# Second layer's first conditioning columns: from beside the first layer's projection to beside its gates

## The chip, the cores and the metric

The kernel runs on one core of one Trainium2 chip. The metric is the device time of one execution in microseconds; less is better. The engines are TensorE (PE in the rows; PEld is its weight load), VectorE (DVE), ScalarE (ACT), GpSimd (POOL) and SyncE (SP), whose queue issues almost all transfers.

## What is computed

A stack of two transformer blocks follows another of two. The change touches the first. Its two layers work on 512 tokens of `x` and 256 of `ctx`, with 1024 columns:

```python
mod_x = (silu(c) @ w_ada[l] + b_ada[l])            # sh1, sc1, g1, sh2, sc2, g2
mod_c = (silu(c_ctx) @ w_ada[l] + b_ada[l])
p_x = modulate(x, sh1, sc1) @ w_in[l]              # keys/values, Fourier, queries, gate logits
g_f, g_m, g_g = split(sigmoid(gate_logits + b_gate), 3)
mix_x = (g_f * y_f + g_m * y_m + g_g * y_g) @ w_o
x = layer_norm(alpha * x + g1 * mix_x, ...)
x = layer_norm(alpha * x + g2 * sq_relu_mlp(modulate(x, sh2, sc2)), ...)
```

`w_ada[l]` is 1024 x 6144. Its six parts of 1024 columns are the six conditioning vectors. Each is needed for `c` and, in the first layer, for `c_ctx`. The second layer's parts 0 and 1 (`sh1`, `sc1`) are first needed at the end of the first layer's MLP.

## The kernel before

**Weight products.** `gemm` (line 313) runs a product as n slots over two ring buffers. In a slot TensorE works through G groups of tokens (the matmuls are line 367). It waits for the slot's weights (`ring_full`), for the pieces of their split (`w_split`), and, before group g, for the eviction of the group `depth` before it (`evac_done`). Each weight is split into a rounded part and a rest, so that three products of fp32r stand for one of fp32: lines 393 and 397 on VectorE, 395 and 397 on GpSimd. SP issues the weights of slot s + 2 when all groups of slot s are done (`mm_done`, lines 326 to 338). All orders are written out by hand; each engine's queue runs in program order.

**Conditioning units.** Most of `w_ada` is multiplied away from `gemm`, by the class `Macs` (line 516). A unit is 512 columns of one part of one layer. It is loaded in four quarters of 512 KB by SP (`load`, line 564) into two buffers: the load of quarter n waits until quarter n - 2 has been used (`mac_freed`). VectorE multiplies and adds a quarter with two k-tiles for each conditioning (`pieces`, line 573), so a unit with both conditionings is 16 operations on 512 columns: two `tensor_scalar` (line 587) and fourteen `scalar_tensor_tensor` (line 589, two inputs in SBUF). TensorE then sums over the partitions (`pe`, line 595): 8 matmuls with one column for the parts that go to columns (16 records, line 607), or a product with a 2-column pick for the parts 2 and 5 that go to rows (line 603). VectorE adds the sum to its place (`take`, lines 619 and 624). Parts 2 and 5 are also stored to memory, with their bias loaded first (lines 540 and 559). SP's part of a unit is the method `sp` (line 542): quarters 2 and 3 of this unit, the store of the unit before, the bias, and then quarters 0 and 1 of the next unit.

**Projection.** `project` (line 804) runs in each layer with four slots of 320 columns (G = 6, weights split by VectorE in four pieces) after a first product with two slots of 272. In the first layer the four slots also carry the four units of the second layer's parts 0 and 1: after a slot's split VectorE takes the unit before and works all four quarters of its own (lines 399 to 401); TensorE sums the unit of the slot before ahead of group 1. The last unit is summed after the last slot, and TensorE waits until it has been added. `fourier` comes next. Ahead of the units' loads SP issues the two loads of `fourier_loads` (2.1 MB).

**Gates.** `gated` (line 1567) runs eight slots. In the first layer G is 6: groups 0 to 2 are the three branches for 512 tokens, groups 3 to 5 for the other 256. A group is 24 fp32r matmuls and 4 of fp32 (8 records). The weights of a slot are six loads, and GpSimd splits them in six pieces of two operations once all six have landed. After each group ScalarE takes the sigmoid (line 1589) and VectorE multiplies and adds (lines 1606, 1608, 1611). `depth` is 3. Each slot carries one unit of the layer's own parts 2 to 5: after group 1 VectorE takes the unit of the slot before and works quarters 0 and 1, after group 2 quarters 2 and 3. TensorE sums the unit of the slot before ahead of group 1. In the second layer G is 3, with one conditioning. The eighth unit is summed and taken in `mix_norm` (line 1665), the output projection.

Of the kernel before, what the change touches and what calls it, by code (L numbers as in the profile page):

```python
# [21 lines left out]
KD = D // P  # L22
# [9 lines left out]
KV_COLS = 256 + ROT + 2 * KVH * HD  # L32
# [4 lines left out]
REST = GATE_COL - KV_COLS  # L37
# [71 lines left out]
def build(nc, A, out):  # L109
    ctx = ExitStack()  # L110
    with ctx:
# [49 lines left out]
        P1 = view(0, NT, GATE_COL)  # L161
# [153 lines left out]
        def gemm(G, mms, evac, depth, split=None, join=True, ready=None, loads=None, macs=None, behind=None, between=None):  # L315
# [5 lines left out]
            n, parts, issue = streams[at_stream[0]]  # L321
            at_stream[0] += 1
            with block(join) as b:
                @b.sync
                def _(sp):
                    for i in range(n // 2 - 1):
                        for s in range(SLOTS):

                            if macs:
                                macs.sp(sp, i * 2 + s)  # L330
                            sp.wait_ge(mm_done.sem, i * (2 * G) + mm_done.n + (s + 1) * G)
                            for d in issue(sp, s, i * 2 + s + 2):
                                d.then_inc(ring_full[s].sem, 16)
                    def free(s):
                        if macs:
                            macs.sp(sp, n - 2 + s)
                        sp.wait_ge(mm_done.sem, mm_done.n + (n - 1 + s) * G)
                    if loads:
                        loads(sp, free)
                    else:  # L340
                        first_loads(sp, free)

                @b.tensor
                def _(pe):
                    def body(i):
                        for s in range(SLOTS):
                            pe.wait_ge(ring_full[s].sem, i * (16 * parts) + ring_full[s].n + 16 * parts)
                            for g in range(G):
                                if ready and i == s == 0:
                                    ready(pe, g)  # L350
                                if between:
                                    between(pe, (i * 2 + s) * G + g)
                                if macs and g == (2 if G == 3 else 1):
                                    macs.pe(pe, i * 2 + s - 1)

# [16 lines left out]
                if split:  # L372
# [4 lines left out]
                    def splitter(eng):  # L377
                        def body(i):
                            for s in range(SLOTS):
# [4 lines left out]
                                for q in range(pieces):  # L384
# [9 lines left out]
                                    elif name[s] == "gpsimd":  # L394
# [3 lines left out]
                                                      ALU.subtract).then_inc(w_split[s].sem, 1)  # L398
                                if macs and name[s] == "vector":
                                    macs.take(eng, i * 2 + s - 1)  # L400
                                    macs.pieces(eng, i * 2 + s, 0, 4)
                                if behind:
# [113 lines left out]
        class Macs:  # L516
# [6 lines left out]
            def __init__(self, units, conds, bank, first=0):  # L523
                self.units, self.conds, self.bank, self.first = units, conds, bank, first
                self.base = Macs.done
                Macs.done += len(units)
                self.rows = {u: sum(p % 3 == 2 for _, p, _ in units[:u]) for u in range(len(units) + 1)}
                self.row_base = mac_stored.n // 16
                mac_stored.n += 16 * self.rows[len(units)]

            def unit(self, slot_index):
# [271 lines left out]

        def project(nt, width, col, dst, join=True, ready=None, macs=None):
            def mms(s, g, d):
# [4 lines left out]
            def evac(b, n):  # L810
                @b.scalar
                def _(act):
# [7 lines left out]
                    loop(n, body)  # L820
            gemm(nt, mms, evac, 4, (("vector", "vector"), KD * width, PROJECT_W, 4), join, ready, None, macs)
            if macs:
                macs.pe(nc.tensor, 3)
                macs.take(nc.vector, 3)
                macs.all_taken(nc.tensor)

# [740 lines left out]
        def gated(l, nq, macs):  # L1567
            halves = [(0, 512), (512, T)] if nq == NT else [(0, 512)]
            G = 3 * len(halves)
# [11 lines left out]
            def evac(b, n):  # L1581
# [12 lines left out]
                def _(dve):  # L1594
                    for i in range(n // 2):
                        for s in range(2):
                            for g in range(G):
# [9 lines left out]
                                else:  # L1607
# [3 lines left out]
                                    dve.tensor_tensor(acc if br == 1 else mix, acc, sig, ALU.add).then_inc(evac_done.sem, 1)  # L1611
                                if g == 1:
                                    macs.take(dve, i * 2 + s - 1)
                                    macs.pieces(dve, i * 2 + s, 0, 2)
                                if g == 2:
                                    macs.pieces(dve, i * 2 + s, 2, 4)
            def ready(pe, g):
# [5 lines left out]
            def loads(sp, free):  # L1623
# [10 lines left out]
                w1_chunk(sp, l, 1, 0)  # L1634
                macs.sp(sp, KD)
            nc.sync.wait_ge(pv_done.sem, pv_done.n)
# [28 lines left out]
        def mix_norm(l, nq, G, macs):  # L1665
# [10 lines left out]
            with block(False) as b:  # L1676
                @b.tensor
                def _(pe):
                    for i, (t, h) in enumerate(order):
# [7 lines left out]
                        if i == 2:  # L1687
                            macs.pe(pe, KD - 1)
                            macs.all_taken(pe)
# [11 lines left out]
                def _(dve):  # L1701
# [24 lines left out]
                    if l == 0:  # L1726
                        residual(1, 0)
                        macs.take(dve, KD - 1)
                        norms(0, residual(0, 1))
                    else:  # L1730
                        i = residual(0, 1)
                        macs.take(dve, KD - 1)
                        norms(0, i)
                        residual(1, 0)
# [1688 lines left out]
        for l in range(DEPTH):  # L3423
            last = l == DEPTH - 1
            nq = XT if last else NT
            def ready(pe, g):
                pe.wait_ge(ht_ready.sem, now.ht + g + 1)
            project(NT, KV_COLS // 2, 0, P1, False, ready)
            early = Macs([(1, part, half) for part in (0, 1) for half in range(2)], 2, 0) if l == 0 else None
            fourier_loads(now)  # L3430
            project(nq, REST // 4, KV_COLS, P1, False, macs=early)
            fourier(nq)
            latents(NT, nq)
            up(NT, nq)
            attend(l, nq)
            macs = Macs([(l, part, half) for part in (2, 3, 4, 5) for half in range(2)], 1 if last else 2, 7)
            G = gated(l, nq, macs)
# [54 lines left out]
```

## Time and profile before

| | us |
|---|---|
| median of 3 runs | 3420.51 (3415.57 to 3423.5) |
| the profiled execution, its own time | 3413.63 |
| its span, first to last instruction | 3411.6 |
| TensorE busy | 3144.0 (92%) |
| VectorE busy | 1984.4 (58%) |
| GpSimd busy | 942.7 (28%) |
| mean granted TensorE clock | 0.961 of full speed |

The span is the time between the first and the last instruction; the execution's own time has 2 us around it. Busy time of TensorE is modelled at its end: matmuls are pipelined, so what counts is the distance from start to start. Of the stretches that the change touches, the first layer's projection ends at 206 us, and the first layer's gates run from 533 to 866 us.

### The profile page before, as it was taken

Reading aid. Unit: us, or ns where it says so; the run is one execution under the profiler, and the core shown is the slowest. Engines: PE = TensorE matmul, PEld = TensorE weight load, DVE = VectorE, ACT = ScalarE, POOL = GpSimd, SP = SyncE. Lnnn points to the kernel's source line nnn. Section 1 sums busy time; section 2 is a strip of 40 time slices with the busy share of each in tenths; the row PEclk is TensorE's granted clock in tenths of the full one; section 3 lists DMA queues with packets and bytes.
Section 4 is the critical chain, followed back from the end, with each engine's and each line's share of the span. In section 5 each row is a group of like instructions: output and inputs, shape, how many; then the busy total and the mean of one; then the engine's idle time right before and its main releaser. Section 6 shows DMA issues by size and latency. Waiting matters only on the chain.

```text
span 3411.6 us, 37992 instructions
## 1 busy us (share of the span) xinstructions
PE 3144.0 (92%) x15196; PEld 2461.1 (72%) x15196; DVE 1984.4 (58%) x3016; ACT 1002.8 (29%) x1749; POOL 942.7 (28%) x708
## 2 busy tenths in 40 slices
PE   6998999999999999989899999899988989989798
PEld 3985666777578888879575665588878856777576
DVE  4576774444665555583677354666665855667344
ACT  3135771000231111141366100322222135431352
POOL 1004766331210000010177654200000325531262
PEclk9999999999999999989899999999999988999799
DMA  6411004343222121123101555132212310023100
GB/s 204 156 53 28 10 29 130 105 108 106 80 75 74 50 74 61 63 80 120 28 1 38 165 162 188 50 115 99 99 51 92 108 50 1 32 80 102 50 1 25
DMA packets 206335, 268.26 MB, mean 79 GB/s; under 512 B 29280, under 2 KB 133680, under 8 KB 205648
## 3 DMA queue, kind: packets, MB, share of 16 engines
q1 hardware_dynamic: 204080, 265.83, 24.2%
q8 instruction: 121, 1.98, 0.2%
q14 instruction: 54, 0.44, 0.0%
q10 hardware_dynamic: 2080, 0.01, 0.0%
HBM read 255.17 MB, written 10.52 MB: 78 GB/s over the span
## 4 chain that ended last, share of the span: by engine, by line
PE 39%; DVE 6%; ACT 2%; POOL 2%; issue 2%; DMA 1%; SPq 0%; DVEq 0%; ACTq 0%; POOLq 0%
PE ps L367 14%; PE ps L1911 5%; PE ps L1921 4%; PE ps L2401 2%; PE ps L1323 2%; PE ps L1306 1%; PE ps L1694 1%; PE ps L2731 1%; PE ps L1276 1%; PE ps L2676 1%; PE ps L1088 1%; PE ps L3085 1%; DVE U L2846 0%; DVE U L1433 0%; PE ps L2690 0%
## 5 line engine op out<-in xcount | busy, mean ns | idle before, releaser
L746 POOL TENSOR_TENSOR ht_lo<-HT,ht_hi 128x1024 fp32r<-128x1024 f32 x28 | 69.3, 2474 | 1071.6 <-DVE X L704 627.0
L1911 PE MATMUL ps<-ht_hi,w_hi 128*128 128x512 f32 (+1 forms) x832 | 286.6, 344 | 18.2 <-POOL ht_lo L746 9.8
L1911 PE MATMUL ps<-ht_lo,w_hi 128*128 128x512 f32 (+1 forms) x832 | 285.2, 343 | 0.0
L1911 PE MATMUL ps<-ht_hi,w_lo 128*128 128x512 f32 (+1 forms) x832 | 285.0, 343 | 0.0
L1921 PE MATMUL ps<-w_hi,a_hi 128*128 128x512 f32 x640 | 251.8, 393 | 4.3 <-DVE a_lo L2036 4.3
L1921 PE MATMUL ps<-w_hi,a_lo 128*128 128x512 f32 x640 | 250.5, 391 | 0.0
L1921 PE MATMUL ps<-w_lo,a_hi 128*128 128x512 f32 x640 | 250.4, 391 | 0.0
L367 PE MATMUL ps<-w_lo,ht_hi 128*128 128x320 f32 (+2 forms) x800 | 244.2, 305 | 0.0
L1490 POOL TENSOR_TENSOR p_lo<-ring,p_hi 128x512 fp32r<-128x512 f32 x156 | 199.9, 1291 | 113.3 <-DVE p_hi L1445 87.5
L367 PE MATMUL ps<-gate_ht_hi,gate_w_hi 128*128 128x512 f32 (+1 forms) x576 | 224.1, 389 | 1.5 <-POOL w_lo L397 1.5
L367 PE MATMUL ps<-U,ring 128*128 128x512 f32 (+1 forms) x576 | 217.9, 521 | 0.0
L589 DVE SCALAR_TENSOR_TENSOR U<-U,stat 128x512 f32<-128x512 f32 x224 | 201.8, 901 | 12.5 <-DMA U<-w_ada_dram 2.7
L367 PE MATMUL ps<-ht_lo,gate_w_hi 128*128 128x512 f32 (+1 forms) x576 | 204.6, 355 | 0.0
L367 PE MATMUL ps<-gate_ht_hi,w_lo 128*128 128x512 f32 (+1 forms) x576 | 204.6, 355 | 0.0
L1589 ACT ACTIVATE U<-ps,bgate 128x512 f32<-128x512 f32 (+1 forms) x72 | 44.4, 616 | 513.6 <-PE ps L367 513.6
L1969 ACT ACTIVATE U<-ps 128x512 f32<-128x512 f32 (+1 forms) x104 | 51.5, 497 | 472.3 <-PE ps L1911 464.7
L1911 PEld LDWEIGHTS ps<-ht_hi,w_hi 128*128 128x128 f32 x832 | 160.1, 192 | 37.5 <-POOL ht_lo L746 10.2
L395 POOL TENSOR_TENSOR gate_w_hi<-ring,cst 128x512 fp32r<-128x512 f32 x96 | 111.6, 1163 | 239.4 <-DMA ring<-w_go_dram 239.4
L1911 PEld LDWEIGHTS ps<-ht_lo,w_hi 128*128 128x128 f32 x832 | 160.2, 193 | 17.9 <-issue 0.2
L1911 PEld LDWEIGHTS ps<-ht_hi,w_lo 128*128 128x128 f32 x832 | 160.0, 192 | 17.5
L2034 DVE TENSOR_TENSOR U<-U 128x512 f32<-128x512 f32 (+1 forms) x104 | 66.9, 643 | 178.9 <-ACT U L1969 178.0
L2049 DVE TENSOR_TENSOR ring<-ps,U 128x512 f32<-128x512 f32 x140 | 96.3, 688 | 117.9 <-PE ps L1921 117.9
(415 smaller groups left out, 8005.0 us busy)
## 6 DMA issues: line engine op xcount, KB each, us to landing
ring<-w_dram SPq DMA_DIRECT2D x30, 2048.0 KB, 8.0
U<-w_ada_dram SPq DMA_DIRECT2D x80, 512.0 KB, 3.7
ring<-w_in_dram SPq DMA_DIRECT2D x48, 512.0 KB, 5.9
ring<-w_in_dram SPq DMA_DIRECT2D x8, 1280.0 KB, 5.8
ring<-a_w_in_dram SPq DMA_DIRECT2D x8, 1280.0 KB, 6.8
ring<-w_ada_dram SPq DMA_DIRECT2D x4, 2048.0 KB, 10.9
hi_scratch<-ht_hi SPq DMA_DIRECT2D x2, 3072.0 KB, 10.0
gate_ht_hi<-hi_scratch SPq DMA_DIRECT2D x8, 768.0 KB, 4.5
```

Source lines behind the costliest of these rows:

```text
L367: last = pe.matmul(ps[0:lhsT.shape[1], bank, 0:cols], lhsT, rhs, start=(k == 0), stop=(k == len(pairs) - 1))
L395: eng.tensor_tensor(h, w, one, ALU.mult).then_inc(w_rounded[s].sem, 1)
L589: ins = dve.scalar_tensor_tensor(acc, w, by, acc, ALU.mult, ALU.add)
L746: pool.tensor_tensor(HT_LO[:, :, tokens], HT[:, :, tokens], HT_HI[:, :, tokens].bitcast(F32), ALU.subtract).then_inc(ht_ready.sem, 1)
L1323: last = pe.matmul(o, lhsT[:, t, :], rhs[:, c], start=(n == 0 and t in (0, XT) and t == (XT if j == 6 else 0)), stop=(n == 2 and t == NT - 1))
L1490: pool.tensor_tensor(PL[g % PB][:, :], PF[g % PB], PH[g % PB][:, :].bitcast(F32), ALU.subtract).then_inc(p_split.sem, 1)
L1911: last = pe.matmul(ps[:, g % 4, 0:c1 - c0], lhsT, rhs, start=(k + j == 0), stop=(k == KD - 1 and j == 2))
L1921: last = pe.matmul(ps[:, 4 + z % 4, :], lhsT, rhs, start=(start and j == 0), stop=(stop and j == len(pairs) - 1))
L1969: act.activation(RELU[:, g % 2, 0:c1 - c0], ps[:, g % 4, 0:c1 - c0], ACT.Relu).then_inc(h_taken.sem, 1)
L2034: dve_chain.link(dve, dve.tensor_tensor(r, r, r, ALU.mult))
L2049: dve_chain.link(dve, dve.tensor_tensor(PROD[h], ps[:, 4 + z % 4, :], G_ROWS[:, 0 if t < XT else 1, h * 512:(h + 1) * 512], ALU.mult))
L2401: last = pe.matmul(ps[:, i * XT + t, :], lhsT, rhs, start=(k == self.order[0] and n == 0), stop=(k == self.order[-1] and n == 2))
```

## The change

The four units of the second layer's parts 0 and 1 are appended to the eight units of the first layer's gates. `Macs` now says by three new methods which units a slot carries and when. With twelve units, slots 0 and 1 carry one each (units 0 and 1), slots 2 to 5 two each (2 and 3, ..., 8 and 9), slots 6 and 7 one each (10 and 11). In a slot with two units VectorE works quarters 0 and 1 of the first after group 0, quarters 2 and 3 after group 1, quarters 0 and 1 of the second after group 3, and 2 and 3 after group 5. TensorE sums the last unit of the slot before ahead of group 1, and the slot's first unit ahead of group 3. SP handles both units ahead of the weights of slot s + 2. The projection no longer carries units. With eight units (second layer) the order is the one of before.

```diff
@@ gemm, SP
-                            if macs:
-                                macs.sp(sp, i * 2 + s)
+                            for u in macs.of(i * 2 + s) if macs else ():
+                                macs.sp(sp, u)
                             sp.wait_ge(mm_done.sem, i * (2 * G) + mm_done.n + (s + 1) * G)
@@ gemm, TensorE
-                                if macs and g == (2 if G == 3 else 1):
-                                    macs.pe(pe, i * 2 + s - 1)
+                                if macs and macs.sums_at(i * 2 + s, g, G) is not None:
+                                    macs.pe(pe, macs.sums_at(i * 2 + s, g, G))
@@ gemm, splitter
-                                if macs and name[s] == "vector":
-                                    macs.take(eng, i * 2 + s - 1)
-                                    macs.pieces(eng, i * 2 + s, 0, 4)
@@ class Macs
+            def of(self, slot):
+                if len(self.units) == KD:
+                    return [slot]
+                return [slot] if slot < 2 else [2 * slot - 2, 2 * slot - 1] if slot < 6 else [slot + 4]
+
+            def sums_at(self, slot, g, G):
+                if g == (2 if G == 3 else 1) and slot:
+                    return self.of(slot - 1)[-1]
+                return self.of(slot)[0] if g == 3 and len(self.of(slot)) > 1 else None
+
+            def beside(self, dve, slot, g):
+                units = self.of(slot)
+                last = self.of(slot - 1)[-1] if slot else -1
+                if len(units) == 1:
+                    if g == 1:
+                        self.take(dve, last)
+                        self.pieces(dve, units[0], 0, 2)
+                    if g == 2:
+                        self.pieces(dve, units[0], 2, 4)
+                elif g in (0, 3):
+                    self.take(dve, units[0] if g else last)
+                    self.pieces(dve, units[g // 3], 0, 2)
+                elif g in (1, 5):
+                    self.pieces(dve, units[g // 5], 2, 4)
@@ project
-            if macs:
-                macs.pe(nc.tensor, 3)
-                macs.take(nc.vector, 3)
-                macs.all_taken(nc.tensor)
@@ gated, VectorE
-                                if g == 1:
-                                    macs.take(dve, i * 2 + s - 1)
-                                    macs.pieces(dve, i * 2 + s, 0, 2)
-                                if g == 2:
-                                    macs.pieces(dve, i * 2 + s, 2, 4)
+                                macs.beside(dve, i * 2 + s, g)
@@ the layers
-            early = Macs([(1, part, half) for part in (0, 1) for half in range(2)], 2, 0) if l == 0 else None
             fourier_loads(now)
-            project(nq, REST // 4, KV_COLS, P1, False, macs=early)
+            project(nq, REST // 4, KV_COLS, P1, False)
...
-            macs = Macs([(l, part, half) for part in (2, 3, 4, 5) for half in range(2)], 1 if last else 2, 7)
+            units = [(l, part, half) for part in (2, 3, 4, 5) for half in range(2)]
+            if not last:
+                units += [(l + 1, part, half) for part in (0, 1) for half in range(2)]
+            macs = Macs(units, 1 if last else 2, 7)
```

In `mix_norm` the index of the last unit becomes `len(macs.units) - 1` on TensorE and VectorE, and `len(macs.units)` in the last `macs.sp` of `gated`'s loads.

## Rows read from the trace of the kernel before

**Rows 1.** the page: busy time, and the costliest conditioning operation

```profile
PE 3144.0 (92%) x15196; PEld 2461.1 (72%) x15196; DVE 1984.4 (58%) x3016; ACT 1002.8 (29%) x1749; POOL 942.7 (28%) x708
...
L589 DVE SCALAR_TENSOR_TENSOR U<-U,stat 128x512 f32<-128x512 f32 x224 | 201.8, 901 | 12.5 <-DMA U<-w_ada_dram 2.7
```

**Rows 2.** stretches: us, then busy us of PE, PEld, DVE, ACT, POOL; clock; DMA

```profile
85.00:210.00 125.00, 117.21 (x816) 116.44 (x815) 70.01 (x105) 14.05 (x34) 0.00 (x0) 0.97 0.44 142
653.90:696.20 42.30, 42.30 (x209) 33.02 (x208) 19.71 (x27) 3.48 (x6) 14.30 (x12) 1.00 0.39 106
```

**Rows 3.** waits of TensorE, 85 to 240 us: total, times, longest

```profile
PE ps L367 <- DVE w_lo L397: 7.5, 1, 7.5
```

**Rows 4.** VectorE's timeline in the projection: start, us, operation, [idle before]

```profile
119.46 1.01 DVE L587 TENSOR_SCALAR U<-U,stat 128x512 f32<-128x512 f32 x2 [21.70 <-DMA U<-w_ada_dram]
...
131.99 0.48 DVE L393 CAST project_w_hi<-ring 128x640 fp32r<-128x640 f32 x1
132.51 0.83 DVE L397 TENSOR_TENSOR w_lo<-ring,project_w_hi 128x640 fp32r<-128x640 f32 x1
```

**Rows 5.** TensorE in the projection, timeline, and a stretch of it with its clock

```profile
133.49 0.61 PE L367 MATMUL ps<-project_w_hi,ht_hi 128*128 128x320 f32 x1 [7.53 <-DVE w_lo L397]
...
204.04 1.84 PE L607 MATMUL ps<-cst,U 128*128 128x1 f32 x16
206.13 2.22 PE L867 MATMUL ps<-X,U 128*128 128x257 f32 x9 [0.25 <-DVE modc L624]
...
133.40:137.40 4.00, 3.92 (x15) 3.94 (x16) 3.62 (x6) 0.00 (x0) 0.00 (x0) 0.50 0.93 332
```

**Rows 6.** the projection's slot-1 weights, issue and landing; page: conditioning loads

```profile
L272 SPq DMA_DIRECT2D ring<-w_in_dram x1: 379/379/379, 104.9 to 104.9; - x1
...
DMA to landing us min/median/max: 5.8/5.8/5.8
...
U<-w_ada_dram SPq DMA_DIRECT2D x80, 512.0 KB, 3.7
```

**Rows 7.** ScalarE's timeline in slot 3 of the gates: TensorE's groups end

```profile
653.89 0.47 ACT L1589 ACTIVATE U<-ps,bgate 128x256 f32<-128x256 f32 x1 [4.13 <-PE ps L367]
662.81 0.69 ACT L1589 ACTIVATE U<-ps,bgate 128x512 f32<-128x512 f32 x1 [8.44 <-PE ps L367]
673.53 0.69 ACT L1589 ACTIVATE U<-ps,bgate 128x512 f32<-128x512 f32 x1 [10.03 <-PE ps L367]
682.42 0.69 ACT L1589 ACTIVATE U<-ps,bgate 128x512 f32<-128x512 f32 x1 [8.20 <-PE ps L367]
```

**Rows 8.** timeline of VectorE in slot 3 of the gates

```profile
676.19 2.61 DVE L587 TENSOR_SCALAR U<-U,stat 128x512 f32<-128x512 f32 x2
...
685.72 6.32 DVE L589 SCALAR_TENSOR_TENSOR U<-U,stat 128x512 f32<-128x512 f32 x8
...
697.18 0.43 DVE L1611 TENSOR_TENSOR U<-U 128x256 f32<-128x256 f32 x1
```

**Rows 9.** timeline of GpSimd in slot 3: first and last of 12

```profile
665.15 1.04 POOL L395 TENSOR_TENSOR gate_w_hi<-ring,cst 128x512 fp32r<-128x512 f32 x1 [28.98 <-DMA ring<-w_go_dram]
...
678.60 1.33 POOL L397 TENSOR_TENSOR w_lo<-ring,gate_w_hi 128x512 fp32r<-128x512 f32 x1
```

**Rows 10.** SP's queue: first and last of the weight loads at slot 3's start

```profile
653.89 2.11 SPq L1560 DMA_DIRECT2D ring<-w_in_dram  x3
...
660.09 0.83 SPq L1562 DMA_DIRECT2D ring<-w_go_dram  x1
```

**Rows 11.** timelines of VectorE and GpSimd in the second layer's gates

```profile
1945.74 6.34 DVE L589 SCALAR_TENSOR_TENSOR U<-U,stat 128x512 f32<-128x512 f32 x4
...
1946.79 1.62 POOL L397 TENSOR_TENSOR w_lo<-ring,gate_w_hi 128x512 fp32r<-128x512 f32 x1
```

**Rows 12.** stretches: a gap of TensorE and what followed

```profile
980.90:984.30 3.40, 0.10 (x2) 0.04 (x1) 2.22 (x1) 3.40 (x3) 2.35 (x1) 0.95 0.00 0
984.30:987.40 3.10, 3.10 (x15) 3.10 (x16) 2.72 (x4) 1.52 (x2) 0.00 (x0) 0.51 0.71 186
```

More of the change, by code:

```diff
@@ L334, in free @@
                     def free(s):
-                        if macs:
-                            macs.sp(sp, n - 2 + s)
+                        for u in macs.of(n - 2 + s) if macs else ():
+                            macs.sp(sp, u)
                         sp.wait_ge(mm_done.sem, mm_done.n + (n - 1 + s) * G)
@@ L802, in build, with project @@
         PROJECT_W = [rounded_view(f"project_w_hi{s}", "U", at_xn + D + s * KD * 320, KD * 320) for s in range(SLOTS)]
-        def project(nt, width, col, dst, join=True, ready=None, macs=None):
+        def project(nt, width, col, dst, join=True, ready=None):
             def mms(s, g, d):
@@ L820, in _ @@
                     loop(n, body)
-            gemm(nt, mms, evac, 4, (("vector", "vector"), KD * width, PROJECT_W, 4), join, ready, None, macs)
-            if macs:
-                macs.pe(nc.tensor, 3)
-                macs.take(nc.vector, 3)
-                macs.all_taken(nc.tensor)
+            gemm(nt, mms, evac, 4, (("vector", "vector"), KD * width, PROJECT_W, 4), join, ready)
         AB = [view(at_ft + 4 * T + 2 * P + i * 2 * S, 2, S) for i in range(2)]
@@ L1634, in loads @@
                 w1_chunk(sp, l, 1, 0)
-                macs.sp(sp, KD)
+                macs.sp(sp, len(macs.units))
             nc.sync.wait_ge(pv_done.sem, pv_done.n)
@@ L1687, in _ @@
                         if i == 2:
-                            macs.pe(pe, KD - 1)
+                            macs.pe(pe, len(macs.units) - 1)
                             macs.all_taken(pe)
@@ L1727, in _ @@
                         residual(1, 0)
-                        macs.take(dve, KD - 1)
+                        macs.take(dve, len(macs.units) - 1)
                         norms(0, residual(0, 1))
@@ L1731, in _ @@
                         i = residual(0, 1)
-                        macs.take(dve, KD - 1)
+                        macs.take(dve, len(macs.units) - 1)
                         norms(0, i)
```

## The prediction

> **What bounds the kernel now.** I read the page first. TensorE works in 92% of the span and VectorE in 58% [rows 1], so VectorE matters only where TensorE waits for it. The costliest conditioning operation lasts 901 ns in the mean [rows 1], though eight in a row take 6.32 us, 0.79 each, when nothing disturbs them [rows 8]: some of them meet something. The change takes VectorE work from one stretch and puts it into another; I read both by the view of stretches [rows 2]. In the stretch from 85 to 210 us, which holds the first layer's projection, TensorE works 117.2 of 125 us; in a slot of the first layer's gates it works all of 42.3 us, while VectorE works 19.7 and GpSimd 14.3. The waits of TensorE in the first stretch have one long entry: 7.5 us for a split of weights on VectorE [rows 3]. VectorE's timeline says why: it stood idle until 119.46 for the first conditioning quarter, then worked off the unit until 132, and only then split the weights of slot 1 [rows 4]. TensorE had finished slot 0 at 126.0 and went on at 133.49, 7.53 later [rows 5].
>
> **What the change removes.**
> 1. That wait: 7.5 us [rows 3]. Without the unit, the split of slot 1 waits only for its weights. They are issued at 104.9, when the product before frees the slot, and landed in 5.8 us [rows 6]; four pieces of about 1.3 us each [rows 4] are done before 117, nine microseconds ahead of TensorE. So nothing takes the place of this wait.
> 2. The slow clock behind it. From 133.5 to 137.4, after this wait, the granted clock was 0.50, 1.2 instead of 2.4 GHz [rows 5]: 3.9 us, half of it lost, 1.9 us.
> 3. The sums. A unit's sums cost TensorE 1.84 us in line [rows 5]. Three stand between matmuls of the projection: 5.5 us. The fourth comes after the last matmul (204.04) and the next stage starts at 206.13. Without it that stage waits for ScalarE's last eviction, which I put at 0.6 us after the matmuls' end at 204.2 (one operation, 0.44 to 0.47 by a like one in [rows 7], and the handover), so 1.4 us are gained.
> Together 7.5 + 1.9 + 5.5 + 1.4 = 16.3 us off. SP's queue in the projection loses sixteen loads, which lets the weights of slots 2 and 3 come sooner; they were hidden, and I count nothing.
>
> **What it adds in the gates.** Four more units pass through them, each 16 operations on VectorE (0.79 us when alone) and one sum on TensorE. The sums cost 4 x 1.84 = 7.4 us, since TensorE has no gap there [rows 2]. The last unit's sum stays at the output projection with another form, taken at nothing. The VectorE operations fit by busy time (19.7 + 13 of 42.3 us), but there are now deadlines inside the slot. I count from the start T of a slot; the one shown has T = 653.9 [rows 7]. TensorE ends group 0 at T + 8.9; a sum and group 1 make it T + 19.6; group 2 ends at T + 28.5 [rows 7]; groups 3 to 5 have half the columns and fill the remaining 13.8 us at 4.6 each. Before group 3 TensorE now waits for all four quarters of the slot's first unit; before group 1 for the second unit of the slot before. Behind either wait stands its whole stream of matmuls, and behind that ScalarE and VectorE. VectorE has a new wait too: after group 0 it takes the unit before, whose sum TensorE forms after its own group 0, at T + 10.8. Behind this wait stand quarters 0 and 1 of the first unit, T + 10.9 to 17.3, done before group 1 ends, so it costs nothing as long as nothing disturbs them.
>
> The second unit's last two quarters come after group 5. VectorE is through with that group's gate 1.4 us after the slot's end (697.6 against 696.2 [rows 8]), and eight operations bring it to 7.8 us after. TensorE asks at 8.9: this deadline holds, by 1.1 us. But SP's queue is held. Its load of the next unit's second quarter waits for the very last quarter, and the six loads of the next weights stand behind it. Before, they were issued as the slot ended (653.89 [rows 10]); now at 8.2 to 8.3 us into the next slot. GpSimd starts 11.3 us after the issue (665.15) and splits until 679.93 [rows 9]. The burst therefore moves from T + 11.3 to T + 19.6 and lasts to T + 34 or more. The weights are due at T + 42 or later, so the lateness itself costs nothing. The loads of quarters 2 and 3 of the unit stand behind the six as well (issuing the six takes SP 7 us, from 653.89 to 660.9 [rows 10], so it is free at T + 15.3); at 3.7 us each [rows 6] they land by about T + 21, in time. In slot 4 (part 5, which goes to rows) SP also stores the first unit and loads the bias of the second after that store has landed; all of it lies before the last quarters' wait and is hidden by it.
>
> What costs is the meeting with GpSimd. Where the two run together, they take turns: in the second layer's gates four of these operations last 6.34 us, 1.585 each, and a split on GpSimd 1.62 [rows 11] instead of 1.3 [rows 9]. In the slot shown the first two lasted 1.3 each instead of 0.5 [rows 4, 8]. **Slots 3, 4 and 5:** quarters 2 and 3 of the first unit start after the gate of group 1, at T + 22.3 (676.19 [rows 8]), and lie inside the burst: 8 x 1.585 = 12.7, ending at T + 35.0. TensorE is ready at T + 28.5: it waits 6.5 us, three times, 19.5 us. **Slot 2:** slot 1 has one unit, so the burst comes at T + 11.3 as before. Quarters 0 and 1 start at T + 11.6 (the unit before goes to a row, a slightly longer addition) and run in it: 2 x 1.3 + 6 x 1.585 = 12.1, to T + 23.7; the gate of group 1 follows until T + 25.3; of the other eight one still meets a piece: 7.0, ending at T + 32.3. TensorE waits 3.8 us. **Slot 6** has one unit but a late burst: quarters 0 and 1 from T + 22.6, 12.1 us in company, the gate of group 2 until T + 36.5, quarters 2 and 3 until T + 42.8, and only then the gate of group 3, for which the next slot's group 0 waits, at T + 43.3, where the slot ended at T + 42.4: 0.9 us. Waits: 3.8 + 19.5 + 0.9 = 24.2 us.
>
> The clock behind these waits is not in the trace of before. The nearest rows are the slow clock above (3.9 us after a wait of 7.5, cost 1.9) and a gap of 3.3 us after which the clock was 0.51 for 3.1 us [rows 12], cost 1.6. The bounds are 0 and 1.9 each. I take 1.6 + 3 x 1.9 = 7.3 us, since the waits are about as long as those of the rows.
>
> **Sum:** 24.2 + 7.3 + 7.4 - 16.3 = 22.6 us slower. The profiled execution took 3413.6 us, so 3436.2 by its own time; the runs' median is 3420.5, 6.9 above it, so I forecast 3443 us.
>
> **Rivals.**
> *A, the quarters are in time (faster).* Place: VectorE's second eight operations before group 3 in slots 2 to 5. If GpSimd gives way rather than VectorE, they last 6.3 us and end at T + 28.6, and TensorE hardly waits. Then -16.3 + 7.4 = -8.9: 3411.6. It decides from the point where waits and clock together stay below 8.9 us, 2.2 a slot. For it: busy shares leave 9 us free on VectorE. Against it stands the second layer [rows 11], where VectorE had its next operation ready every time and still took turns. The Trainium skill ("SBUF — State Buffer", Who interferes with whom) says that a VectorE instruction with two inputs in SBUF holds a read port shared with GpSimd exclusively, and that the order of issue decides who is blocked, the other fully. Were VectorE always first, this case would follow and the sum be -8.9; by turns it is +22.6. The trace has turns (1.585 against 0.79). Chance 0.10.
> *B, half the price.* The burst meets only half of the eight: 4 x 1.585 + 4 x 0.79 = 9.5, a wait of 3.3 in slots 3 to 5 and 2 in slot 2, clock 5: 12 + 5 + 7.4 - 16.3 = +8, 3428.6. It takes weights that land later or sooner than I think by 6 us. Chance 0.15, split about evenly over the bound to "no change".
> *C, loads late too.* Quarter 2 is issued behind 2.3 MB of weights. The first conditioning load of the projection, issued behind 3.3 MB, was awaited until 119.46 [rows 4]. If it lands at T + 27.5, five of eight operations meet GpSimd: 5 x 1.585 + 3 x 0.79 = 10.3, ending at T + 37.8, 2.8 more in three slots: 3452. Chance 0.12.
> *D, the first wait stays* because the weights of slot 1 are late: 9 us worse, 3452. Their landing time speaks against it. Chance 0.03.
> My forecast has 0.60.
>
> **Range and chances.** A measurement can tell about 0.2%, 6.8 us, so "same" is 3413.7 to 3427.3. The bounds of the clock (0 to 7.6 for four) and the scatter of the runs around the forecast give 3434 to 3448; B and C extend that to 3424 and 3456. A lies outside. Faster 0.10, same 0.09, slower 0.81.
>
> **What would show it.** In the profile after: no wait for the split in the projection, matmuls at full clock there, and the next stage starting near 190 instead of 206. In the gates: TensorE waiting for VectorE's quarters in slots 2 to 5 before group 3, 6 to 7 us in three of them; SP's weight loads 8 us after a slot's end; GpSimd's bursts starting 19 to 20 us into slots 3 to 6; conditioning operations near 1.6 us in them; slots of about 50 us instead of 42.3. The forecast is wrong if those operations stay at 0.79, if the bursts stay at T + 11, or if the gates get longer by no more than the sums.

## The result and the profile after

The changed kernel takes 3442.14 us (median of 4 runs) beside 3419.11 before: a ratio of 1.0068, 95% interval 1.0054 to 1.0082. Repeated later with six runs it took 3442.78 beside 3418.14: 1.0070 (1.0056 to 1.0084). The change costs 23 to 25 us. The forecast was 3443: 22.6 us on top of 3420.5, the median of before as known then from three runs.

First the projection. TensorE's timeline at the first matmul with 320 columns, before:

```profile
104.67 0.31 PE L367 MATMUL ps<-project_w_hi,ht_hi 128*128 128x320 f32 x1
```

In the changed kernel, at the same matmul and at the start of the next stage:

```profile
106.61 0.31 PE L367 MATMUL ps<-project_w_hi,ht_hi 128*128 128x320 f32 x1
...
191.87 7.17 PE L888 MATMUL ps<-X,U 128*128 128x257 f32 x32 [0.62 <-ACT U L843]
```

From the one to the other it takes 85.3 us; before, the same stretch went from 104.67 to 206.13 [rows 5 have its end], 101.5 us. That is 16.2 us less. The wait for the split [rows 3] and the 1.84 us of each sum are gone; the next stage now waits 0.62 us for ScalarE's last eviction, as expected (0.6).

Then the gates. The view of stretches by slot, slots 1 to 7 (columns as in [rows 2]: length, then busy PE, PEld, DVE, ACT, POOL, clock, DMA share, GB/s), against 42.3 us and a clock of 1.00 in [rows 2]:

```profile
551.70:594.20 42.50, 42.50 (x198) 31.39 (x197) 18.99 (x27) 3.49 (x6) 14.23 (x12) 1.00 0.38 106
594.20:646.80 52.60, 47.69 (x214) 36.23 (x213) 31.61 (x36) 3.49 (x6) 18.09 (x12) 0.94 0.37 101
646.80:701.20 54.40, 47.75 (x226) 38.10 (x225) 35.76 (x44) 3.49 (x6) 17.54 (x12) 0.91 0.42 121
701.20:754.30 53.10, 46.41 (x214) 33.60 (x213) 36.03 (x44) 3.49 (x6) 17.54 (x12) 0.94 0.42 121
754.30:807.70 53.40, 47.55 (x214) 36.09 (x213) 35.40 (x44) 3.49 (x6) 17.74 (x12) 0.94 0.43 128
807.70:850.00 42.30, 42.30 (x208) 32.64 (x207) 28.72 (x31) 3.50 (x6) 17.42 (x12) 1.00 0.41 113
850.00:896.00 46.00, 44.19 (x210) 34.45 (x210) 19.21 (x32) 3.49 (x6) 0.00 (x0) 0.96 0.25 89
```

Slots 2 to 5 take 52.6, 54.4, 53.1 and 53.4 us, slot 7 46.0. In slots 2 to 5 TensorE stands idle for 5 to 7 us, VectorE works 32 to 36 us instead of 19.7 and GpSimd 17.5 to 18 instead of 14.3. In slots 3 to 5 VectorE's share has grown by 16 us, where a unit brings 13, and GpSimd was given nothing new. The waits of TensorE in the gates (in total, times, longest):

```profile
PE ps L632 <- DVE U L614: 17.4, 3, 6.7
PE ps L628 <- DVE U L614: 6.7, 1, 6.7
PE ps L367 <- issue: 1.8, 1, 1.8
```

Four waits for the quarters (line 614 is 589 of before), 24.1 us; the fifth, 1.8 us, is the start of slot 7, for which the profile names no releaser; VectorE began the gate of group 3 that it waits for at 851.3, when the last quarters of slot 6 were done. Slot 3 in the timelines of TensorE, VectorE, GpSimd and SP's queue:

```profile
682.00 3.57 PE L632 MATMUL ps<-cst,U 128*128 128x1 f32 x16 [6.65 <-DVE U L614]
...
669.38 12.57 DVE L614 SCALAR_TENSOR_TENSOR U<-U,stat 128x512 f32<-128x512 f32 x8
...
702.60 6.33 DVE L614 SCALAR_TENSOR_TENSOR U<-U,stat 128x512 f32<-128x512 f32 x8
...
667.86 1.04 POOL L395 TENSOR_TENSOR gate_w_hi<-ring,cst 128x512 fp32r<-128x512 f32 x1 [43.83 <-DMA ring<-w_go_dram]
...
684.61 1.27 POOL L397 TENSOR_TENSOR w_lo<-ring,gate_w_hi 128x512 fp32r<-128x512 f32 x1
...
654.93 3.56 SPq L1581 DMA_DIRECT2D ring<-w_in_dram  x3
...
709.37 3.42 SPq L1581 DMA_DIRECT2D ring<-w_in_dram  x3
```

The slot starts at 646.9. SP issues its weight loads at 654.93, 8.0 us later (before: 0.0 [rows 10]). GpSimd's twelve operations run from 667.86 to 685.9, 21.0 us into the slot (before 11.3 [rows 9]). The eight operations of quarters 2 and 3 start at 669.38 and take 12.57 us where [rows 8] have 6.32. TensorE waits 6.65 us until 682.0, and the sum then lasts 3.57 us instead of 1.84 [rows 5]. The slot ends at 701.3. Only then, from 702.60 to 708.9, come the second unit's last quarters, and behind them, at 709.37, SP's next weight loads.

### The profile page after: what moved, and what is told of

Read it like the earlier page. It is cut to its first block, busy times and chain, and to the rows that moved or that the text cites. A ratio compares the mean times of both kernels' runs of the same rounds, so it can differ in the third digit from the quotient of the medians.

```text
span 3439.3 us, 37991 instructions
## 1 busy us (share of the span) xinstructions
PE 3154.5 (92%) x15196; PEld 2467.2 (72%) x15196; DVE 2013.8 (59%) x3016; ACT 1004.2 (29%) x1749; POOL 961.2 (28%) x708
## 4 chain that ended last, share of the span: by engine, by line
PE 39%; DVE 6%; ACT 2%; POOL 2%; issue 2%; DMA 1%; SPq 0%; DVEq 0%; POOLq 0%; ACTq 0%
PE ps L367 14%; PE ps L1928 5%; PE ps L1938 4%; PE ps L2418 2%; PE ps L1344 2%; PE ps L1327 1%; PE ps L1711 1%; PE ps L2748 1%; PE ps L1297 1%; PE ps L2693 1%; PE ps L1109 1%; PE ps L3102 0%; DVE U L2863 0%; PE ps L3054 0%; DVE U L1454 0%
## 5 line engine op out<-in xcount | busy, mean ns | idle before, releaser
L614 DVE SCALAR_TENSOR_TENSOR U<-U,stat 128x512 f32<-128x512 f32 x224 | 232.0, 1036 | 10.0
L395 POOL TENSOR_TENSOR gate_w_hi<-ring,cst 128x512 fp32r<-128x512 f32 x96 | 122.7, 1278 | 276.1 <-DMA ring<-w_go_dram 276.1
L1928 PEld LDWEIGHTS ps<-ht_hi,w_lo 128*128 128x128 f32 x832 | 159.9, 192 | 17.5
```

The lines of the kernel that those rows point to most:

```text
L395: eng.tensor_tensor(h, w, one, ALU.mult).then_inc(w_rounded[s].sem, 1)
L614: ins = dve.scalar_tensor_tensor(acc, w, by, acc, ALU.mult, ALU.add)
L1928: last = pe.matmul(ps[:, g % 4, 0:c1 - c0], lhsT, rhs, start=(k + j == 0), stop=(k == KD - 1 and j == 2))
```

## The experiments

Each was timed in rounds with the kernel before on the same chip. "Gates" below is the time from the end of slot 1 to the end of slot 7, from the starts of ScalarE's sigmoids: 254.3 us before, 301.8 in the changed kernel. The two sigmoids of before, and behind them those of the changed kernel:

```profile
611.38 0.47 ACT L1589 ACTIVATE U<-ps,bgate 128x256 f32<-128x256 f32 x1 [4.13 <-PE ps L367]
865.72 0.47 ACT L1589 ACTIVATE U<-ps,bgate 128x256 f32<-128x256 f32 x1 [4.13 <-PE ps L367]
...
594.26 0.47 ACT L1610 ACTIVATE U<-ps,bgate 128x256 f32<-128x256 f32 x1 [4.13 <-PE ps L367]
896.04 0.47 ACT L1610 ACTIVATE U<-ps,bgate 128x256 f32<-128x256 f32 x1 [4.13 <-PE ps L367]
```

### Partial sums in PSUM

```diff
-   w, by, acc = MAC_W[q % 2][:, i, :], sil[...], MAC_ACC[:, c, :]
+   w, by, acc = MAC_W[q % 2][:, i, :], sil[...], ps[:, 6 + c, :]
...
-   ins = dve.scalar_tensor_tensor(acc, w, by, acc, ALU.mult, ALU.add)
+   to = MAC_ACC[:, c, :] if q == 3 and i == 1 else acc
+   ins = dve.scalar_tensor_tensor(to, w, by, acc, ALU.mult, ALU.add)
```

(and ahead of the output projection's first product TensorE waits for the last unit's quarters, which are long done.)

> The changed kernel, with the partial sums of a unit kept in two PSUM banks that are free in the gates (6 and 7) instead of in SBUF; only the unit's last two operations write to SBUF. The number, order, size and deadlines of VectorE's operations, and all transfers, stay as they are; what goes is the second SBUF input of fourteen of the sixteen operations. Theory 1 (VectorE and GpSimd take turns, and that alone makes the first unit late): the operations last about 0.8 us also while GpSimd splits weights, quarters 2 and 3 end near 28.5 us into the slot, and the four waits ahead of group 3 (4.9 to 6.7 us in the changed kernel's trace) fall below 1 us each, with the slow clock behind them. The time is 3402 to 3411 us. Rival (too many operations before the deadline, whatever GpSimd does): the waits stay at 4 us or more, 3435 us or more. Rival (the quarters' loads are late behind the weights): the waits stay, and VectorE is seen waiting for loads.

Measured: 3412.88 us, ratio to before 0.9978 (0.9964 to 0.9991). The waits of TensorE for quarters in the gates:

```profile
PE ps L629 <- DVE U L615: 0.5, 1, 0.5
PE ps L633 <- DVE U L615: 0.5, 1, 0.5
```

Slot 3's quarters 2 and 3 in VectorE's timeline, and two of GpSimd's operations beside them:

```profile
666.38 4.77 DVE L615 SCALAR_TENSOR_TENSOR ps<-U,stat,ps 128x512 f32<-128x512 f32 x6
671.18 1.53 DVE L615 SCALAR_TENSOR_TENSOR U<-U,stat,ps 128x512 f32<-128x512 f32 x2
...
668.69 1.27 POOL L397 TENSOR_TENSOR w_lo<-ring,gate_w_hi 128x512 fp32r<-128x512 f32 x1
669.91 1.04 POOL L395 TENSOR_TENSOR gate_w_hi<-ring,cst 128x512 fp32r<-128x512 f32 x1
```

Eight operations take 6.3 us in the middle of the burst, and GpSimd's take 1.27 and 1.04 instead of some 1.6 and 1.5. The 24.1 us of waits are 1.0. No operation, deadline or load was moved (the two `tensor_scalar` that open a unit have even become slower, 1.54 us instead of 1.01 when undisturbed), so theory 1 holds and both rivals fall: not the number of operations and not the loads made the first unit late, but the second SBUF input beside GpSimd. The time is 1.9 us above the expected range; the gates take 264.7 us (599.29 to 863.98), 3.0 more than the sums explain: of these 1.0 are waits and 1.7 go to a stretch of 3.4 us at 1.2 GHz in slot 3, after a wait of 0.45 us.

### First unit summed ahead of group 4

```diff
-   return self.of(slot)[0] if g == 3 and len(self.of(slot)) > 1 else None
+   return self.of(slot)[0] if g == 4 and len(self.of(slot)) > 1 else None
```

> The changed kernel, with one number changed: TensorE sums a slot's first unit ahead of group 4 instead of group 3. VectorE's operations and their meeting with GpSimd stay. Theory 1: quarters 2 and 3 still end 35 us into the slot, but TensorE asks at 33.1 instead of 28.5, so the waits shrink by 4.6 us each, to 0.3 in slot 2 and about 2 in slots 3 to 5, and waits that short leave the clock at its upper level; slot 7's 1.8 stays. 25.9 us of waits become about 8, of some 14 us of slow clock about 11 go: 3442 - 29 = 3413 us. Rival (VectorE has more in the slot than fits): what is saved ahead of group 4 comes back ahead of group 1 of the next slot, and the time stays above 3430 us.

Measured: 3420.62 us, ratio 1.0007 (0.9991 to 1.0022): the loss is gone, the gain has not come.

```profile
PE ps L632 <- DVE U L614: 3.5, 3, 1.9
...
PE ps L628 <- DVE U L614: 2.1, 1, 2.1
PE ps L367 <- issue: 1.9, 1, 1.9
```

5.6 us of waits for the quarters and 1.9 at slot 7, 7.5 where 8 were expected, and the gates take 275.0 us instead of 301.8. The rival falls: nothing comes back ahead of group 1. The expected time was missed by 7 us, the gates' part of it (26.8 us of 29) by 2; the rest isn't in the stretches that the edit touches. The waits that are left of some length are 1.87, 2.10 and 1.27 us in slots 3 to 5 and 1.94 at slot 7; three of the four, all but the one of slot 4, still had 3.4 us at 1.2 GHz behind them.

### Weight loads first in SP's queue

```diff
-   for u in macs.of(i * 2 + s) if macs else ():
-       macs.sp(sp, u)
+   us = macs.of(i * 2 + s) if macs else ()
+   for u in us:
+       # the last argument: issue quarters 0 and 1 of the next unit too; not for the second unit
+       macs.sp(sp, u, u == us[0] and len(us) > 1 or len(us) == 1)
    sp.wait_ge(mm_done.sem, ...)
    for d in issue(sp, s, i * 2 + s + 2): ...
+   if len(us) > 1:
+       macs.ahead(sp, us[1])                  # quarters 0 and 1 of the next unit
```

> The changed kernel, with SP's queue reordered in the slots with two units: the six weight loads are issued when the slot ends, and the next unit's quarters 0 and 1 behind them instead of ahead. Theory 1: GpSimd's burst moves back to 11 us into each slot, and now meets quarters 0 and 1 and the gate of group 1 instead of quarters 2 and 3; slots 3 to 5 become like slot 2, with a wait of about 4.9 us instead of 5.8 to 6.7, and the wait at the start of slot 7 (1.8) goes. Waits fall from 25.9 to about 20, the time by 6 to 10 us, to about 3434 us. Rival (the held weight loads are the cost): the waits ahead of group 3 go in slots 3 to 5, and the time falls by 25 us or more, to 3417 us or less.

Measured: 3441.53 us, ratio 1.0060 (1.0036 to 1.0083). TensorE's waits ahead of group 3 in slots 3 and 5, and VectorE in slot 5:

```profile
678.38 3.57 PE L641 MATMUL ps<-cst,U 128*128 128x1 f32 x16 [4.70 <-DVE U L623]
...
784.85 3.58 PE L641 MATMUL ps<-cst,U 128*128 128x1 f32 x16 [6.76 <-DVE U L623]
...
763.26 2.56 DVE L621 TENSOR_SCALAR U<-U,stat 128x512 f32<-128x512 f32 x2 [2.44 <-DMA U<-w_ada_dram]
```

The waits are 4.92, 4.70, 4.86 and 6.76 us, and none at slot 7. The first three are what theory 1 says of a burst that starts 10 us into the slot; in slot 5 VectorE stood 2.44 us for a quarter that was now behind the weights, which is rival C of the prediction in small. The gates take 296.7 us, 5.1 less: slot 7 gives 3.7, slots 3 and 4 give 1.1 and 2.2, and slot 5 takes 1.9 back. So the held weight loads are not the main cost: where the burst lies matters by 2 us a wait in slots 3 and 4. The expected 3434 us was missed; in the total the 5 us are not to be told from chance.

### The four units left out

```diff
-   if not last:
-       units += [(l + 1, part, half) for part in (0, 1) for half in range(2)]
```

> The four units of the second layer's parts 0 and 1 are left out altogether (neither beside the projection nor beside the gates), so this conditioning is not computed: the removal alone, without the addition. Theory 1: what is removed from the projection is worth 16.3 us against the kernel before (17.1 by the two traces up to the gates), and nothing of it comes back later: 3402 to 3403 us. Rival (the projection's gain is partly taken back by the next stages, which wait for something else): 3407 us or more.

Measured: 3403.22 us, ratio 0.9956 (0.9940 to 0.9973). This is 15.4 us below the kernel before on the same chip, where 16.3 were expected. The gates take 254.3 us, as before. The removal is worth what the forecast says, and little of it comes back.

### Both: PSUM and the later sum

> The changed kernel with both edits: partial sums in PSUM, and the first unit summed ahead of group 4. With PSUM alone quarters 2 and 3 ended within 0.5 us of TensorE's question, and one wait of 0.45 us was followed by a slow clock. Theory 1: the later question leaves 4 us to spare, no wait and no slow clock is left in the slots, every slot with two units takes 44.2 us, and the time is 3409 us or 1 to 4 us below PSUM alone (3405 to 3413), faster than the kernel before by 0.2 to 0.3%. If the addition still cost something besides the sums (4 x 1.84 us), the gates would be longer than 8 x 42.3 + 7.4 us.

Measured: 3410.91 us, ratio 0.9975 (0.9962 to 0.9988). Slots 2 and 3 by stretches:

```profile
593.30:637.60 44.30, 44.30 (x213) 33.19 (x212) 24.59 (x36) 3.48 (x7) 14.09 (x12) 1.00 0.44 123
637.60:681.70 44.10, 44.10 (x225) 34.81 (x224) 30.75 (x44) 3.48 (x7) 14.50 (x12) 1.00 0.52 150
```

The columns say: TensorE busy throughout, clock 1.00, and GpSimd back at 14.1 to 14.5 us. No wait, no slow clock, 44.1 to 44.3 us a slot, and the gates take 261.7 us: 254.3 and 7.4 for four sums. By the medians this is the fastest kernel of the study that computes everything, though its difference to PSUM alone (2 us) is within the intervals.

### The kernel before, with PSUM

> The kernel before, with the partial sums of the units beside the gates in PSUM and nothing else changed: a control for the PSUM edit. Theory 1: in the kernel before TensorE waits for none of these operations, so freeing them and GpSimd from each other changes nothing: within 0.1% of the kernel before (about 3419 us). Rival (the PSUM form brings time of its own, for instance in the second layer's gates, where the two also meet): 3412 us or less, and then the change with PSUM would owe its time to that.

Measured: 3423.39 us, ratio 1.0015 (1.0003 to 1.0027); the gates take 254.3 us to the tenth, and the second layer's gates, which the edit touches too, 211.6 us from the first sigmoid to the last in both kernels. The PSUM form brings nothing of its own. If anything this kernel is slower, by somewhat more than the expected 0.1%, and neither stretch that the edit touches shows why; in its profile the first sigmoid of the gates already comes 7.0 us later than before (544.30 instead of 537.28), ahead of the first edited operation. The gain of the two kernels above is the change's.

### The kernel before, with the split ahead of the unit

```diff
     # gemm's splitter, after the split of slot i * 2 + s
-    macs.take(eng, i * 2 + s - 1)
-    macs.pieces(eng, i * 2 + s, 0, 4)
+    macs.take(eng, i * 2 + s - 2)              # from slot 1 on
+    macs.pieces(eng, i * 2 + s - 1, 0, 4)
...
     # TensorE: the sum of the unit of the slot before
-    if macs and g == (2 if G == 3 else 1):
+    if macs and g == (3 if macs.bank == 0 else 2 if G == 3 else 1):
```

(and the last unit's quarters after the last slot.)

> The kernel before, with VectorE's order in the projection changed: it splits the weights of slot s + 1 before it works the unit of slot s, and TensorE sums a unit ahead of group 3 of the next slot; the four units stay beside the projection and the gates are untouched. Theory 1: the wait of 7.5 us and the slow clock behind it (1.9) go, the sums stay; at the projection's end TensorE now waits 1 to 2 us for the last unit. The next stage starts near 198 us instead of 206, and the time falls by about 8 us, to 3411 us. Rival (the wait only moves, to a later split or to the last unit): no gain, 3419 us.

Measured: 3411.65 us, ratio 0.9978 (0.9966 to 0.9991). The end of the projection on TensorE:

```profile
198.94 3.58 PE L607 MATMUL ps<-cst,U 128*128 128x1 f32 x16 [3.65 <-DVE U L589]
202.77 7.41 PE L869 MATMUL ps<-X,U 128*128 128x257 f32 x22 [0.26 <-DVE modc L624]
```

The wait of 7.5 us is gone and one of 3.65 stands at the end, with a slow sum behind it (3.58 us). The stretch takes 97.5 us (105.31 to 202.77) instead of 101.5, 4.0 less where about 8 were expected: the last unit was done at 198.9 instead of 196, since VectorE had waited for its loads too, and the clock fell once more. By the medians the kernel is 5.5 us below the one before. The rival (the wait only moves) is half right: part of the wait has come back at the end, and half of the expected 8 us is kept. With the units where they were, this kernel comes within 1 us of the fastest one here, inside the intervals.

### TensorE kept at work while it waits

```diff
+   if macs and g == 3 and len(macs.of(i * 2 + s)) > 1:
+       for lhsT, rhs in mms(s, 0, 0)[0][2]:    # 24 matmuls of 512 columns, result unused
+           pe.matmul(ps[:, 6, 0:512], lhsT, rhs, start=True, stop=True)
```

> The changed kernel, with 24 more matmuls on TensorE ahead of group 3 in the slots with two units (the products of group 0 once more, into an unused bank, their result read by nobody): 5.3 us of work where it waited 4.9 to 6.7 us. Theory 1, on the slow clock: the clock falls because TensorE stands idle. Filled, the waits are 1.3 us or less, no slow clock follows, the sums ahead of group 3 last 1.84 us instead of 3.5, and slots 3 to 5 take 50.7 to 51 us instead of 53.1 to 54.4; the time falls by 8 to 12 us, though TensorE does 21 us more work: about 3432 us. Rival (the clock falls for another reason, or the fill only adds): the slots stay at 53 us or grow, 3442 us or more.

Measured: 3438.55 us, ratio 1.0050 (1.0035 to 1.0065). The sum ahead of group 3 in slots 2 and 3 on TensorE's timeline:

```profile
628.36 1.84 PE L635 MATMUL ps<-cst,U 128*128 128x1 f32 x16
...
679.14 1.95 PE L635 MATMUL ps<-cst,U 128*128 128x1 f32 x16 [1.04 <-DVE U L617]
```

Slot 3 in the view of stretches:

```profile
644.20:695.00 50.80, 49.76 (x249) 39.20 (x248) 35.61 (x44) 3.45 (x6) 17.63 (x12) 1.00 0.45 130
```

With 21 us more to do, TensorE is through the gates in 289.0 us instead of 301.8. The clock stays at 2.4 GHz, the sums last 1.84 to 1.95 us again, and slots 3 to 5 take 50.9 to 51.1 us. The quarters end at the same time (in slot 3 the sum starts 35.0 us into the slot, 35.1 without the fill). So some 12.8 us of the change's loss in the gates are slow clock, and the clock falls because TensorE stands idle. The total fell by 4 us by the medians, less than the 8 to 12 expected, and the intervals of the two ratios overlap; for the clock the stretches decide, not the total.

### Both kernels again

> The changed kernel once more, unchanged. Its first profile showed the gates 47.6 us longer than before and the projection 16.2 us shorter, 31.4 us in sum, while the medians differ by 23.0. Theory 1 (the forecast's terms for waits and slow clock were too small, and the medians' 23 us owes some to chance in the rest of the program): the gates come out at 296 to 303 us from the end of slot 1, and the difference of the medians nearer to 28 us. Rival (the first profile had more slow clock than most executions): 292 to 295 us, and the medians differ by 22 to 24 us again.

> The kernel before once more, unchanged, for its profile: the projection takes 101.5 us again from its first matmul with 320 columns to the next stage's first, the gates 254.2 us from the end of slot 1. The rest behind the gates, the same program in all kernels, comes out anywhere between 2543 and 2557 us; 2546 as in the first profile would say that it depends on the kernel and not on chance.

The changed kernel's second profile: gates 301.5 us (594.35 to 895.89), the projection's stretch 85.3, own time 3446.2; the medians differ by 24.6 us. The kernel before: gates 254.3, projection 101.8, own time 3412.9, behind the gates 2543.3. Neither alternative fits well. The gates come out as in the first profile, so the rival (an unusual first profile) falls, but the medians stay nearer to 24 than to 28.

## Why the prediction was right, and where it owes something to chance

**What the change removes: right, term by term.** Expected 16.3 us; the stretch is 16.2 shorter, and leaving the units out altogether gains 15.4 by the medians. The split of slot 1 found nothing else to wait for.

**The sums: right.** With all waits gone the gates are 7.4 us longer.

**SP's queue and the burst: right.** The loads come 8.0 us into the slot (8.2 to 8.3 expected) and the burst at 21.0 instead of 19.6. But the weight experiment shows that this step was worth only some 2 us a wait, and the 1.8 us at slot 7: a burst at T + 11 also costs waits of 4.7 to 4.9 us.

**The turns: right, and shown.** The quarters take 12.57 us for eight operations (12.7 expected), waits of 4.9, 6.65, 6.7 and 5.8 us (3.8, 6.5, 6.5, 6.5), 1.8 at slot 7 (0.9): 25.9 in sum against 24.2. The PSUM kernel takes the turns away and moves nothing else, and the waits fall to 1.0. The rule of the Trainium skill ("SBUF — State Buffer", Who interferes with whom), that a VectorE instruction with at most one input in SBUF, outside the two-port modes, does not contend with GpSimd, is borne out by it: 0.79 us each beside GpSimd at full speed. Its clause on the order of issue would have given rival A only if VectorE always came first; the trace has turns.

**The slow clock: half of what it is.** This is the mis-sized term. I took 1.6 to 1.9 us a wait, 7.3 in sum, and bounded it by 1.9. It is 12.8 to 14: the gates are 47.4 us longer, of which waits make 25.9 and sums 7.4, which leaves 14.1 (13.8 by the second profile), and the filled kernel gives back 12.8 with the same end of the quarters. The prediction's own terms make a slot of 42.3 + 1.84 + 6.5 + 1.9 = 52.5 us, not the "about 50" that it names as a sign; measured are 52.6 to 54.4. I had read the row behind it [rows 5] without the stretch ahead of it, which shows the wait of the kernel before itself:

```profile
126.00:133.40 7.40, 0.00 (x0) 0.00 (x0) 6.97 (x11) 0.43 (x1) 0.00 (x0) 0.81 0.54 148
```

The mean clock of 0.81 says that 2.8 of these 7.4 us were already at half clock: part of the slow stretch had passed inside the wait and cost nothing, and 1.9 us is what the other part cost. In slots 2, 3 and 5 of the changed kernel more of it falls on work. In slot 2 the clock was at its upper level all through the wait of 4.9 us in the first profile, and the sum and group 3 behind it took 9.8 us instead of 6.4. A shorter wait was not a cheaper one.

But the length of the wait does not settle the price either. Slots 3 and 4 have nearly the same wait (6.65 and 6.69 us), with the clock at half for some 2.5 to 2.8 us of it in both. The stretches are the wait and what followed at half clock, for slot 3 and then for slot 4:

```profile
675.30:682.00 6.70, 0.05 (x1) 0.00 (x0) 6.49 (x6) 0.69 (x1) 6.54 (x5) 0.79 0.26 78
682.00:689.20 7.20, 7.20 (x33) 7.20 (x34) 1.60 (x2) 0.00 (x0) 3.80 (x3) 0.50 0.25 73
729.70:736.40 6.70, 0.08 (x1) 0.00 (x0) 6.49 (x6) 0.69 (x1) 6.54 (x5) 0.81 0.27 78
736.40:740.50 4.10, 4.03 (x6) 0.87 (x7) 1.42 (x3) 0.00 (x0) 2.50 (x2) 0.50 0.40 128
```

Behind the wait of slot 3 the clock stayed low for 7.2 us, behind that of slot 4 for 4.1. What TensorE did first differs: in slot 3 the sum is sixteen records of one column, in slot 4, whose unit goes to rows, four records of 512 columns. The price of the slow clock in a slot is its length less its length before, the wait and the sum. In three profiles (changed, changed again, weights first) it is 3.3 to 4.5 us for the nine waits with the one-column sum behind them and 1.9 to 2.4 us for the three with the 512-column sum, close to the 1.9 us of the wait before with its 320-column matmuls. The rows that I went by were as cheap as the latter. No run changes the form of the sum alone, so that it is the cause is not shown.

**The sum.** By the two stretches the change costs 47.4 - 16.2 = 31.2 us, the forecast's own terms put right. The medians say 23.0 and 24.6, and the forecast was 22.6; 31.2 lies above the intervals of both measurements (18 to 28 and 19 to 29 us). For seven of the other kernels the same sum of two stretches and the difference of the medians agree within 3.3 us (all but the kernel before with PSUM, where they are 5.5 apart). What makes up the difference here isn't settled. From the stage after the projection to the end of slot 1 the profiles take 405.3 and 406.4 us before, 402.4 and 404.3 changed. Behind the gates, where the two kernels run the same program but for the form of the last unit's sum, they take 2545.9 and 2543.3 before, 2543.3 and 2548.4 changed; over all the kernels of the study this part lies between 2542 and 2557. And the two profiled executions of the kernel before (3413.6 and 3412.9) were 5 us below the medians of its runs, those of the changed kernel (3441.3 and 3446.2) 1 below and 3 above theirs. That the forecast came within 1 us is therefore partly chance; sign and mechanism are not. The terms that were measured add up to 7 to 8 us more than the medians show, and the clock term that I had 7 us too small happened to make up for that.

**The rivals.** A (quarters in time) did not come, but it is what the PSUM kernels do: 3411.6 was worked out for it, 3410.9 and 3412.9 are measured. A late load, as in C, was seen once, in the weights-first kernel. B and D did not occur.

## What to carry to other kernels

Work that fits an engine by its busy share can still miss a deadline inside a slot: before moving it, lay its operations on the slot's timeline, together with what GpSimd does at that time. A VectorE operation with two SBUF inputs took twice its time beside GpSimd's elementwise work; an accumulator in a free PSUM bank took that away without moving anything. And where an engine's queue order makes one wait, as VectorE's unit ahead of the next split here, turning that order round may give as much as moving the work to another stage.

## What was not expected of the hardware

The price of an idle TensorE is not proportional to the wait. Behind waits of 4.7 to 6.8 us slow clock cost 1.9 to 4.5 us each, in these profiles less where the sum with 512 columns came first than where the sum with one column did. Three of four waits of 1.3 to 2.1 us still brought 3.4 us at 1.2 GHz (sum ahead of group 4), and in one place a wait of 0.45 us did, while one of 0.46 in the same profile did not. Nor is the price fixed from one execution to the next: behind the wait of 1.8 us at slot 7 slow clock cost 1.7 us in the first profile of the changed kernel and nothing in the second. Giving TensorE 21 us of useless matmuls instead of waiting shortened the gates by 12.8 us.
